# Twenty-four modulation chunks evaluated two by two: a case on one Trainium2 core

## The reference, cut to what matters

```python
for i in range(DEPTH):                                # DEPTH = 2
    mod   = jax.nn.silu(c)     @ mod_w[i] + mod_b[i]  # mod_w: (2, 1024, 6144)
    mod_c = jax.nn.silu(c_ctx) @ mod_w[i] + mod_b[i]
    sh1, sc1, g1, sh2, sc2, g2 = jnp.split(mod[:, None, :], 6, axis=-1)
    ...
```

## Time and profile before

| | us |
|---|---|
| median of 3 runs | 2853.32 |
| lowest and highest run | 2851.34 and 2853.95 |
| the profiled execution | 2854.93 |
| its span, first to last instruction | 2853.7 |

### The profile page before, as it was taken

One profiled execution on the slowest core, in us unless ns is written; L12 is line 12 of the kernel. 1 busy time (PEld: TensorE's weight loads), 2 busy tenths in 40 slices (PEclk: granted clock), 3 DMA queues, 4 the chain that ended last, 5 costly groups with the idle time before them and its releaser, 6 DMA issues.

```text
span 2853.7 us, 57760 instructions
## 1 busy us (share of the span) xinstructions
PE 2542.8 (89%) x23928; PEld 1845.7 (65%) x23928; DVE 1225.2 (43%) x2829; ACT 591.3 (21%) x1406; POOL 177.3 (6%) x346
## 2 busy tenths in 40 slices
PE   8999999998999999999998889987758997777776
PEld 7857778666857778668865566665546465544444
DVE  6564455646664455654566211111114253333223
ACT  3211322113211322122145211110002241000001
POOL 0001000010001000020000122221220000000000
PEclk9999999999999999999999999999879998999989
DMA  8744466456744467534040389999994125999997
GB/s 283 231 169 128 167 224 212 172 178 216 231 162 127 164 227 236 207 121 162 1 177 3 151 342 395 408 417 420 420 356 171 59 111 233 418 420 420 418 420 302
DMA packets 271390, 690.40 MB, mean 242 GB/s; under 512 B 35983, under 2 KB 163774, under 8 KB 254782
## 3 DMA queue, kind: packets, MB, share of 16 engines
q1 hardware_dynamic: 259904, 675.42, 63.1%
q0 software_dynamic: 7552, 10.76, 1.1%
q10 hardware_dynamic: 3710, 0.99, 0.2%
HBM read 670.09 MB, written 17.04 MB: 241 GB/s over the span
## 4 chain that ended last, share of the span: by engine, by line
PE 74%; DMA 13%; DVE 7%; issue 3%; ACT 2%; SPq 0%; ACTq 0%; POOL 0%; POOLq 0%; DVEq 0%
PE ps L762 19%; DMA arena<-in_moe_w_up 12%; PE ps L849 9%; PE ps L2957 5%; PE ps L2006 3%; PE ps L3460 3%; PE ps L1892 3%; PE ps L2932 2%; PE ps L2972 2%; PE ps L1257 2%; PE ps L2712 2%; PE ps L3421 1%; PE ps L3484 1%; PE ps L895 1%; PE ps L3436 1%
## 5 line engine op out<-in xcount | busy, mean ns | idle before, releaser
L762 PE MATMUL ps<-arena 128*128 128x256 f32 x2464 | 554.6, 382 | 9.7 <-DVE arena L1051 6.5
L762 PEld LDWEIGHTS ps<-arena 128*128 128x128 f32 x2464 | 462.3, 190 | 92.3 <-issue 13.0
L1002 DVE TENSOR_TENSOR arena<-arena 128x1024 f32<-128x1024 f32 x176 | 214.9, 1223 | 144.2 <-PE ps L762 75.7
L849 PE MATMUL ps<-arena 128*128 128x512 f32 x616 | 266.1, 592 | 0.0
L2957 PE MATMUL ps<-arena 128*32 128x128 f32 x6016 | 196.7, 290 | 64.3 <-issue 61.9
L2957 PEld LDWEIGHTS ps<-arena 128*32 128x32 f32 x6016 | 181.8, 117 | 73.4 <-issue 69.5
L3460 PE MATMUL ps<-arena 128*32 128x128 f32 x4096 | 143.6, 300 | 76.6 <-issue 74.8
L849 PEld LDWEIGHTS ps<-arena 128*128 128x128 f32 x616 | 115.8, 189 | 144.4 <-issue 124.7
L3460 PEld LDWEIGHTS ps<-arena 128*32 128x32 f32 x4096 | 129.4, 121 | 85.0 <-issue 83.2
L3017 DVE TENSOR_TENSOR arena<-arena,ps 128x128 f32<-128x128 f32 x47 | 13.6, 288 | 315.5 <-ACT arena L2987 315.5
L2932 PE MATMUL ps<-arena 128*32 128x256 f32 x1536 | 101.4, 390 | 11.5 <-issue 8.3
(11 more groups left out here) (525 smaller groups left out, 3477.6 us busy)
## 6 DMA issues: line engine op xcount, KB each, us to landing
arena<-in_moe_w_gate SPq DMA_DIRECT2D x64, 2048.0 KB, 26.4
arena<-in_moe_w_up SPq DMA_DIRECT2D x64, 2048.0 KB, 25.2
arena<-in_moe_w_down SPq DMA_DIRECT2D x64, 2048.0 KB, 29.9
arena<-in_mod_w SPq DMA_DIRECT2D x24, 2048.0 KB, 14.0
arena<-in_w_gate SPq DMA_DIRECT2D x44, 1024.0 KB, 5.5
arena<-in_w_up SPq DMA_DIRECT2D x44, 1024.0 KB, 8.8
arena<-in_w_down SPq DMA_DIRECT2D x44, 1024.0 KB, 5.0
arena<-in_w_in SPq DMA_DIRECT2D x12, 1024.0 KB, 5.4
```

The source lines that it names most:

```text
L762: last = pe.matmul(out, tokens[j][:, t, :], weights[t], start=(t == 0 and j in ("P1", "P5", "P6", "P7")), stop=(t == HK - 1), skip_group_c ...
L849: pe.matmul(ps[:, DN_BANK[j], :], rows[j], w, start=(p == 0), stop=(p == CHUNKS - 1), skip_group_check=True).then_inc(*dn.up(l, f, p, j))
L1002: V.tensor_tensor(out, a, b, op).then_inc(*s["w_sum"].up(l, f, c, i))
```

## The change

Two successive chunks `m` (even) and `m + 1` (odd) now share one PSUM bank. Behind `k.cs` stand two more columns, and a second view of the same memory, `k.cs_next`, begins two columns earlier, so that in it the two vectors are columns 2 and 3 of each block. The odd chunk's product uses this view and adds onto what the even chunk's left, which has zeros in those rows: rows 32g to 32g+3 then hold both chunks. One ACT copy takes the bank. Four transposes turn it, where two times four matmuls with `sel` did. VectorE adds the four groups by two `tensor_reduce` from PSUM and, behind a wait for both, the bias for 8 columns at once. Within an FFN the even chunk's place keeps its product alone; copy, turn and sum stand in the odd chunk's place only. All arrays behind `cs` in SBUF move by 2 elements (8 bytes).

```diff
-        self.cs = self.take(KT, 32)
-        self.offset = {"slots": self.top, "raw": self.top - 256 - 512 - 512 - 256 - 1024 - 512 - 1 - 512}
+        both = self.take(2 + KT * 32)
+        self.cs_room = both
+        self.cs, self.cs_next = (both[:, at:at + KT * 32].rearrange("p (k c) -> p k c", k=KT) for at in (2, 0))
+        self.offset = {"slots": self.top, "raw": self.top - 258 - 512 - 512 - 256 - 1024 - 512 - 1 - 512}
...
@@ act_prepare (and the same in act_ffn)
-    for i, (ml, m) in enumerate(mods_before(l, name)):
+    for ml, m in mods_before(l, name)[-1:]:
         act.wait_ge(*s["mod_product"].at(ml, m))
-        act.activation(mod_row_between(k, i), k.ps[:, 2 + i, :], ACT.Copy).then_inc(*s["mod_row"].up(ml, m))
+        act.activation(mod_row_between(k), k.ps[:, 2, :], ACT.Copy).then_inc(*s["mod_row"].up(ml, m))
@@ pe_between
-    for i, (ml, m) in enumerate(mods_before(l, name)):
-        pe_modulate(k, ml, m, m % 2, 2 + i)
+    for ml, m in mods_before(l, name):
+        pe_modulate(k, ml, m, m % 2, 2)
@@ pe_turn_between (dve_between likewise)
-    for i, (ml, m) in enumerate(mods_before(l, name)):
-        pe_modulation_out(k, ml, m, TURN_BANK[name], mod_row_between(k, i), 8 * i)
+    for ml, m in mods_before(l, name)[-1:]:
+        pe_modulation_out(k, ml, m, TURN_BANK[name], mod_row_between(k))
@@ pe_ffn, chunk
-            if mod % 6:
+            if mod % 2 == 0 and mod % 6:
                 pe.wait_ge(*s["mod_out"].at(l, mod - 1))
             pe_modulate(k, l, mod, mod % 2, MOD_BANK)
...
-        if mod is not None:
-            pe_modulation_out(k, l, mod, MOD_BANK, k.mrow, 0)
+        if mod is not None and mod % 2:
+            pe_modulation_out(k, l, mod, MOD_BANK, k.mrow)
@@ pe_modulate
+    cs = k.cs_next if m % 2 else k.cs
     for t in (0, 2, 4, 6, 1, 3, 5, 7):
         g = t // 2
-        last = pe.matmul(k.ps[32 * g:32 * g + 32, bank, :], k.cs[:, t, :], k.mslots[slot][:, t, :], start=(t % 2 == 0), stop=(t % 2 == 1),
+        last = pe.matmul(k.ps[32 * g:32 * g + 32, bank, :], cs[:, t, :], k.mslots[slot][:, t, :], start=(m % 2 == 0 and t % 2 == 0), stop=(m % 2 == 1 and t % 2 == 1),
                          tile_position=(0, 32 * g), skip_group_check=True)
@@ pe_modulation_out
     for q in range(4):
-        last = pe.matmul(k.ps[:, bank, at + 2 * q:at + 2 * q + 2], row[:, q * P:(q + 1) * P], k.c["sel"], start=True, stop=True, skip_group_check=True)
+        last = pe.transpose(k.ps[:, bank, q * P:(q + 1) * P], row[:, q * P:(q + 1) * P], k.c["ident"])
@@ dve_modulation_out
-    to = l * 48 + m * 4
-    V.tensor_tensor(k.mod[:, to:to + 4, :], k.ps[:, bank, at:at + 8].rearrange("p (a b) -> p a b", a=4),
-                    k.cols2[:, 1, to:to + 4].unsqueeze(2).broadcast_to([P, 4, 2]), ALU.add).then_inc(*s["mod_out"].up(l, m))
+    to = l * 48 + (m - 1) * 4
+    parts = k.ps[:, bank, :].rearrange("p (q g c) -> p q c g", q=4, g=4)
+    for i in range(2):
+        V.tensor_reduce(k.mod[:, to + 4 * i:to + 4 * i + 4, :], parts[:, :, 2 * i:2 * i + 2, :], AX, ALU.add).then_inc(*s["mod_summed"].up(l, m, i))
+    V.wait_ge(*s["mod_summed"].last())
+    V.tensor_tensor(k.mod[:, to:to + 8, :], k.mod[:, to:to + 8, :],
+                    k.cols2[:, 1, to:to + 8].unsqueeze(2).broadcast_to([P, 8, 2]), ALU.add).then_inc(*s["mod_out"].up(l, m))
```

More of the change, by code:

```diff
@@ L72 @@
     "dve_setup": "setup_out_dve rope_step cols_out lam_step ready_eps ready_cs0", "dve_norm": "post_paired post_recip post_scaled added norm_recip h_ready",
-    "dve_ffn": "t_sum w_sum u_sum hid_done r_added r_recip y_sum y_bias y_recip y_diag mod_out", "dve_mixer": "mx_dve", "dve_ple": "ple_p_out ple_scaled ple_done",
+    "dve_ffn": "t_sum w_sum u_sum hid_done r_added r_recip y_sum y_bias y_recip y_diag mod_summed mod_out", "dve_mixer": "mx_dve", "dve_ple": "ple_p_out ple_scaled ple_done",
     "dve_tokens": "t_gain t_recip t_normed", "dve_project": "pr_cos pr_sin pr_out kv_tokens kv_sum kv_u", "dve_values": "v_out_dve",
@@ L435, in dve_setup @@
     V.memset(k.eps, EPS).then_inc(*s["ready_eps"].up())
-    V.memset(k.cs, 0.0).then_inc(*s["ready_cs0"].up())
+    V.memset(k.cs_room, 0.0).then_inc(*s["ready_cs0"].up())
     dve_rows(k, "x", 0)
@@ L621, in dve_between, with mod_row_between @@
         k.nc.vector.wait_ge(*k.s["mod_turned"].at(*mods[-1]))
[L622 to L627, removed]
+    for ml, m in mods[-1:]:
+        dve_modulation_out(k, ml, m, TURN_BANK[name])
+def mod_row_between(k):
+    return k.hid[:, 0:2, :].rearrange("p a b -> p (a b)")
 def dve_finish_norm(k, l, name):
@@ L892, in pe_modulate, with pe_modulation_out @@
     pe.wait_ge(*s["cs_ready"].at())
+    cs = k.cs_next if m % 2 else k.cs
     for t in (0, 2, 4, 6, 1, 3, 5, 7):
         g = t // 2
-        last = pe.matmul(k.ps[32 * g:32 * g + 32, bank, :], k.cs[:, t, :], k.mslots[slot][:, t, :], start=(t % 2 == 0), stop=(t % 2 == 1),
+        last = pe.matmul(k.ps[32 * g:32 * g + 32, bank, :], cs[:, t, :], k.mslots[slot][:, t, :], start=(m % 2 == 0 and t % 2 == 0), stop=(m % 2 == 1 and t % 2 == 1),
                          tile_position=(0, 32 * g), skip_group_check=True)
     last.then_inc(*s["mod_product"].up(l, m))
-def pe_modulation_out(k, l, m, bank, row, at):
+def pe_modulation_out(k, l, m, bank, row):
     pe, s = k.nc.tensor, k.s
@@ L903, in pe_modulation_out, with dve_modulation_out @@
     for q in range(4):
-        last = pe.matmul(k.ps[:, bank, at + 2 * q:at + 2 * q + 2], row[:, q * P:(q + 1) * P], k.c["sel"], start=True, stop=True, skip_group_check=True)
+        last = pe.transpose(k.ps[:, bank, q * P:(q + 1) * P], row[:, q * P:(q + 1) * P], k.c["ident"])
     last.then_inc(*s["mod_turned"].up(l, m))
-def dve_modulation_out(k, l, m, bank, at):
+def dve_modulation_out(k, l, m, bank):
     V, s = k.nc.vector, k.s
     V.wait_ge(*s["mod_turned"].at(l, m))
-    to = l * 48 + m * 4
-    V.tensor_tensor(k.mod[:, to:to + 4, :], k.ps[:, bank, at:at + 8].rearrange("p (a b) -> p a b", a=4),
-                    k.cols2[:, 1, to:to + 4].unsqueeze(2).broadcast_to([P, 4, 2]), ALU.add).then_inc(*s["mod_out"].up(l, m))
+    to = l * 48 + (m - 1) * 4
[5 more added lines that the diff above has]
+                    k.cols2[:, 1, to:to + 8].unsqueeze(2).broadcast_to([P, 8, 2]), ALU.add).then_inc(*s["mod_out"].up(l, m))
 def act_ffn(k, l, f, gain, x_ready):
@@ L949, in act_ffn @@
         if c == 0:
-            for i, (ml, m) in enumerate(mods_before(l, name)):
+            for ml, m in mods_before(l, name)[-1:]:
                 act.wait_ge(*s["mod_product"].at(ml, m))
-                act.activation(mod_row_between(k, i), ps[:, 2 + i, :], ACT.Copy).then_inc(*s["mod_row"].up(ml, m))
+                act.activation(mod_row_between(k), ps[:, 2, :], ACT.Copy).then_inc(*s["mod_row"].up(ml, m))
             act.wait_ge(*s["r_summed_up"].at(l, f))
@@ L1130, in chunk @@
             dve_chunk_sum(k, l, f, ahead, 4)
-        if mods_of(l, f, c) is not None:
-            dve_modulation_out(k, l, mods_of(l, f, c), MOD_BANK, 0)
+        if mods_of(l, f, c) is not None and mods_of(l, f, c) % 2:
+            dve_modulation_out(k, l, mods_of(l, f, c), MOD_BANK)
         V.wait_ge(*gu.at(l, f, c, "P4"))
@@ L1664, in pe_ple @@
     pe.wait_ge(*s["p_in"].at(l))
-    pe.wait_ge(*s["mod_row"].at(*mods_before(l, "ple")[0]))
+    pe.wait_ge(*s["mod_row"].at(*mods_before(l, "ple")[-1]))
     for t in range(2):
```

## The result

| | before | changed |
|---|---|---|
| median, us | 2853.32 | 2837.55 |
| lowest and highest run | 2849.16 and 2855.01 (5 runs) | 2833.76 and 2841.63 (5 runs) |
| the profiled execution | 2854.93 | 2838.77 |
| its span | 2853.7 | 2837.6 |
| mean granted TensorE clock | 0.964 | 0.966 |

The ratio is 0.995, 95% interval 0.9937 to 0.9964: 15.8 us faster, where 13.85 was worked out.

The account below looks back on a forecast made before the run. PE work was taken to bound the kernel, with FFNs never leaving PE. Savings of 5.0 + 2.3 + 2.7 + 2.5 + 1.35 = 13.85 us off 2853.3 gave 2839.5 us, range 2835.5 to 2846.

Parts of the forecast that it names:

- Even places: Five even chunks inside FFNs: the turn goes entirely, 5 x 1.00 = 5.0 us saved.
- two readings of a turn's price: One chunk's old turn with `sel`: 1.00 us between weight loads, 0.79 by the chain; 1.00 was taken.
- Odd places: Five odd chunks inside FFNs: turn falls from 1.00 to 0.54 us, 0.46 each, 2.3 us saved.
- Mixers: Two pairs ahead of the mixers: turn falls from 1.89 to 0.54 us, 1.35 each, 2.7 us saved.
- the rival that they land when they did: Transfers between mixer and FFN set their own time, losing gains before 1005 us: 4.6 saved, 2848.7 us; chance 0.08.
- ple: Two pairs in ple: turn falls from 1.78 to 0.54 us, 1.24 each, 2.5 us saved.
- The forecast's sentence that these transfers are issued on PE's progress and move along: Between mixer and FFN, path transfers are issued when PE's output product is done, so they move too.
- Openings: Three pairs opening FFNs: PE could gain 1.47 us each, but VectorE's square sums leave 0.45, 1.35 us saved.
- VectorE's steps hidden: Two reductions and an addition on VectorE, about 0.16 us each, from below 0.16, from above 0.69; both ends cost nothing inside FFNs.
- The clock: Rival: clock falls behind each of 12 transpose groups, losing 20.4 us; 6.6 us slower, 2859.9 us; chance 0.05.
- the forecast's own signs of being wrong: Slow loads behind transposes, longer DMA pieces, granted clock under 1.00 in FFN stretches that had 1.00, gain shrinking after 1300 us.
- To the end: After 1300 us SP's queue waits for PE or VectorE, so the memory-bound stage begins earlier by the same amount.

Follow-up runs that it names:

- `pair_sel`: Changed kernel with each pair turned by four matmuls with a four-column `sel` and two bias additions, instead of transposes and reductions: 2837.3 us, ratio 0.9952.
- `shift_only`: Kernel before with only the arrays behind the context columns moved by 2 elements (8 bytes): 2850.0 us, ratio 0.9993.
- the repeat: The changed kernel measured once more, with no further edit, beside runs of the kernel before: 2839.0 us, ratio 0.9951.
- doubled pairs: Kernel before with the four matmuls of every turn issued twice, so 32 small instructions in a row between stages: 2888.4 us, ratio 1.0124.
- `before_ffn_four`: Kernel before with each turn inside an FFN issued four times over, 32 small instructions in a row, pairs between layers unchanged: 2901.4 us, ratio 1.0177.

## Why the prediction was right

Point by point, with the local steps of the traces (which leave out the clock and the transfers):

- **Even places**: 5.0 forecast, 0.90 to 0.93 each measured, 4.6. Of the two readings of a turn's price, 1.00 by weight loads and 0.79 by the chain, the truth lies between, since a turn also slows the products behind it by 0.12 (7.04 against 6.92, in the chains of `pair_sel` and of the change).
- **Odd places**: 2.3 forecast; 0.46 each by the chunk's length, 2.3. Between landmarks these steps are 0.48 to 0.58, 2.7 in all.
- **Mixers**: 2.7 forecast; 1.30 and 1.22 from the pair's product to the transfer, 2.5. The two transfers behind them lasted 7.90 and 8.10 us against 9.28 and 7.93: they moved along, and the rival that they land when they did is out.
- **ple**: 2.5 forecast. From the turn's start to the end of the projection 1.4 each, 2.8. In ple 0, 1.2 of it was lost at once to the load of the next FFN's weights. The forecast's sentence that these transfers are issued on PE's progress and move along held between mixer and FFN and failed here: the issue began 5.6 earlier but lasted 1.2 longer, and a load that was hidden before became the late one.
- **Openings**: 1.35 forecast, held down by VectorE; 0.5 to 0.6 each, 1.75, and the wait at L872 is 1.01 where 1 was forecast.
- **VectorE's steps hidden**: 0.184 a reduction and 0.28 for both, near the lower bound of 0.16; doubled they still cost nothing.
- **The clock** did not fall behind transposes, not even behind 48. One of the forecast's own signs of being wrong did appear, a clock under 1.00 where an FFN had 1.00: the 24 products at 386.37 took 6.88 against 5.43. But they stand ahead of the turn, which begins at 393.09, and right behind a wait of 2.16 us. The Trainium skill (TensorE: Matmul & The Clock Gate, Part 4: PE-mode transpose) says that transposes do not count as PE work for the clock gate in the same way; the stretch of 5.24 us at 1.00 does not show that in this kernel. What does lower the clock here is the very form that the change removes: in rows of 32, and in ple in three of six rows of 16.
- **To the end**: the lead of 13.84 at the second block became 16.18. Other traces with the same program there gained 0.2 or 6, and `shift_only`, with no change on PE at all, 7.8; it is the second block's own spread.

The local gains add to 4.6 + 2.3 + 2.5 + 2.8 + 1.75 = 13.95, less 1.2 in ple 0: 12.75. The measured 15.8 exceeds that by 3, within the interval of the ratio (10 to 18 us) and what the runs of one kernel differ by; the repeat's 12.9 falls on it. So the mechanism and its price were right, with every term within 0.4 us; that the second block's lead met the forecast to a hundredth was luck.

## What to carry to other kernels

Price a PE piece by how far it moves the next weight load, not by an instruction's duration: four transposes in a row cost 0.54 us and each further four 0.44, though one lasts 272 ns. When a gain shortens PE ahead of a wait, look at once at which engine or load comes next: here VectorE's order gave back 3.0 to 5.1 us for one moved call, and one load took 1.2. A difference of 2 us in 2850 is decided at landmarks in the trace, since the end carries whatever the clock did.

## What the runs showed of the hardware

Rows of 32 small float32 matmul instructions (128x2 out, each behind a 128x128 weight load) lowered the granted clock from 2.4 to 1.2 GHz while PE was never idle, at thirteen of seventeen places (all seven doubled pairs, six of the ten fourfold turns), for 1.7 to 3.4 us of loss each. Rows of 8 and of 16 inside the FFNs did at none of ten places each. Rows of 16 in ple, behind a wait of 0.75 us, did at three of six (the traces of before, `shift_only` and `before_ffn_four`); ahead of the mixers and in the openings of these three they did at none of fifteen. Rows of 48 transposes, of the same weight loads but 128 columns wide, did at none of twelve, though they last longer (5.24 us against 3.5 to 5.0). So neither the number of instructions nor the row's length alone is what the chip reacts to; whether it is the width or the kind of instruction was not separated, since both changed together.
